# RWKV block: receptances projected last, decays summed on TensorE, preparation folded into the projections

## What is computed

```python
xx = pad(x)[:, :-1] - x                       # the token before, minus this one
xr, xw, xk, xv, xa, xg = [x + xx * mu[i] for i in range(6)]
r, k, v = xr @ w_rkv[0], xk @ w_rkv[1], xv @ w_rkv[2]
w = -softplus(-(w_decay0 + tanh(xw @ w_decay1) @ w_decay2)) - 0.5
a = sigmoid(a0 + (xa @ a1) @ a2)
g = sigmoid(xg @ g1) @ g2
kk = heads(k * k_k);  kk = kk * rsqrt(max(sum(kk * kk), 1e-24))
k = k * (1 + (a - 1) * k_a)
decay = exp(-exp(w))                          # = exp(-c * sigmoid(...)), c = exp(-0.5)
S = S * decay + (S @ -kk) (kk * a)^T + v k^T  # per token and head; y = S @ r
y = groupnorm(y) + sum(r * k * r_k) * v       # the second term is the "bonus"
out = (y * g) @ w_o
```

## Time and profile before

| | |
|---|---|
| median of 3 runs | 2507.64 us |
| profiled execution | 2511.72 us, its span 2509.9 us |
| mean granted TensorE clock | 0.902 |
| PE busy over the span | 2208.5 us, 88% |
| DVE, ACT, POOL busy | 891.5, 981.8, 903.5 us |
| chain that ended last | PE 51%, DVE 8%, ACT 3% |

### The profile page before, as it was taken

One profiled execution on the slowest core, in us unless ns is written; L12 is line 12 of the kernel. 1 busy time (PEld: TensorE's weight loads), 2 busy tenths in 40 slices (PEclk: granted clock), 3 DMA queues, 4 the chain that ended last, 5 costly groups with the idle time before them and its releaser, 6 DMA issues.

```text
span 2509.9 us, 31732 instructions
## 1 busy us (share of the span) xinstructions
PE 2208.5 (88%) x12568; PEld 1736.1 (69%) x12570; DVE 891.5 (36%) x1895; ACT 981.8 (39%) x1833; POOL 903.5 (36%) x582
## 2 busy tenths in 40 slices
PE   5999799999976799963799779999897899999898
PEld 4898666778744567632688467888687657888687
DVE  2100366320076455078243544333104063334301
ACT  3331177442353444332234335344225264434312
POOL 2332066444312233342000343544443393454443
PEclk9988599999997799956589889999999899999999
DMA  4322000133300222201100122333322202333322
GB/s 118 85 63 76 18 27 1 60 78 104 89 18 17 63 63 78 61 1 28 32 26 10 44 84 76 93 93 101 103 98 67 76 2 75 93 93 95 106 91 77
DMA packets 222421, 162.13 MB, mean 65 GB/s; under 512 B 31450, under 2 KB 206114, under 8 KB 222274
## 3 DMA queue, kind: packets, MB, share of 16 engines
q1 hardware_dynamic: 219762, 151.91, 20.6%
q0 software_dynamic: 2512, 8.19, 1.1%
HBM read 154.83 MB, written 5.24 MB: 64 GB/s over the span
## 4 chain that ended last, share of the span: by engine, by line
PE 51%; DVE 8%; ACT 3%; issue 2%; POOL 2%; DMA 1%; POOLq 1%; DVEq 0%; ACTq 0%; SPq 0%; PEld 0%; PEldq 0%
PE ps L358 11%; PE ps L329 8%; PE ps L328 8%; PE ps L332 8%; PE ps L368 5%; PE ps L2594 2%; PE ps L2552 2%; POOL buffer L2070 1%; ACT buffer L2649 1%; POOLq L2910 1%; DVE buffer L2220 1%; PE ps L2617 1%; PE ps L2243 1%; PE ps L2564 1%; POOL weights_lo L270 1%
## 5 line engine op out<-in xcount | busy, mean ns | idle before, releaser
L270 POOL TENSOR_TENSOR weights_lo<-buffer,weights_hi 128x1024 fp32r<-128x1024 f32 (+1 forms) x265 | 656.8, 2481 | 1030.9 <-ACT weights_hi L259 1030.5
L259 ACT ACTIVATE weights_hi<-buffer 128x1024 fp32r<-128x1024 f32 (+1 forms) x265 | 276.0, 1045 | 319.6 <-PE ps L368 310.7
L328 PE MATMUL ps<-u_hi,weights_hi 128*128 128x512 f32 (+1 forms) x752 | 281.5, 378 | 6.4 <-DVE u_lo L644 5.9
L329 PE MATMUL ps<-u_lo,weights_hi 128*128 128x512 f32 (+1 forms) x752 | 285.1, 383 | 0.0
L1801 ACT ACTIVATE buffer<-ps,buffer 128x512 f32<-128x512 f32 x88 | 68.4, 777 | 282.6 <-PE ps L332 282.6
L332 PE MATMUL ps<-u_hi,weights_lo 128*128 128x512 f32 (+1 forms) x752 | 176.7, 378 | 0.0
L1831 DVE SCALAR_TENSOR_TENSOR buffer<-ps,buffer,buffer 128x511 f32<-128x511 f32 x88 | 66.1, 751 | 291.9 <-ACT buffer L1801 291.9
L328 PEld LDWEIGHTS ps<-u_hi,weights_hi 128*128 128x128 f32 x752 | 143.4, 191 | 33.2 <-DVE u_lo L644 6.5
L329 PEld LDWEIGHTS ps<-u_lo,weights_hi 128*128 128x128 f32 x752 | 143.1, 190 | 29.3
L2649 ACT ACTIVATE buffer<-ps 32x128 f32<-32x128 f32 (+4 forms) x240 | 92.5, 392 | 177.4 <-PE ps L2594 60.8
L332 PEld LDWEIGHTS ps<-u_hi,weights_lo 128*128 128x128 f32 x752 | 136.6, 190 | 26.6 <-POOL weights_lo L270 0.3
(11 more groups left out here) (371 smaller groups left out, 4588.7 us busy)
## 6 DMA issues: line engine op xcount, KB each, us to landing
buffer<-in_w_up SPq DMA_DIRECT2D x88, 512.0 KB, 3.8
buffer<-in_w_down SPq DMA_DIRECT2D x44, 512.0 KB, 3.2
buffer<-in_diff_w_in SPq DMA_DIRECT2D x32, 512.0 KB, 4.1
buffer<-in_nsa_w_in SPq DMA_DIRECT2D x28, 512.0 KB, 3.7
buffer<-in_w_rkv SPq DMA_DIRECT2D x24, 512.0 KB, 3.7
buffer<-in_nsa_w_out SPq DMA_DIRECT2D x8, 512.0 KB, 3.5
buffer<-in_diff_w_out SPq DMA_DIRECT2D x8, 512.0 KB, 3.5
buffer<-in_norm_g POOLq DMA_DIRECT2D x8, 512.0 KB, 4.3
```

The source lines that it names most:

```text
L259: self.nc.scalar.activation(self.part_hi[:, part % self.PARTS, 0:n], self.raw[:, ld % self.RAW, 0:n], ACT.Copy).then_inc(self.hi_ready, 1)
L270: self.nc.gpsimd.tensor_tensor(self.part_lo[:, part % self.PARTS, 0:n], self.raw[:, ld % self.RAW, 0:n], self.part_hi[:, part % self.PARTS ...
L328: nc.tensor.matmul(out, hi[:, k, :], rhs[0][:, k, tokens], start=(k == 0), stop=False)
L329: nc.tensor.matmul(out, hi[:, k, :], rhs[1][:, k, tokens], start=False, stop=False)
```

## The change

RwkvPrepare and RwkvDecay are gone; RwkvProject goes straight into RwkvCore.

- The order of projections is now decay, key, a, gate, the two second layers, values, receptances. The mixes have buffers laid out anew, so that the value mix does not share one with the mix before it.
- The decay's second layer is made token-major (65 rows: the bias comes as a row of weights beside a row of ones), so that the prefix sums can be products with a constant triangle matrix less the middle's (`C_SUMS`), made by TensorE straight into PSUM. ScalarE takes both exponents from PSUM into PSUM banks 6 and 7, and the products read them there.
- The values come in two halves of 512 features, 4 loads each. `project_tokens` calls `between` after each load: 32 two-column products give the decay sums at the chunk middles (`mids`), 32 more the squared norms (`squares`).
- The receptance tiles come last. Ahead of each, TensorE makes that tile's decay sums (4 products) and spreads the inverse norms over 64 features each (8 products). VectorE makes all products but kk * a, which stays on GpSimd.
- The bonus sums move into the core: GpSimd makes r * k at its start, TensorE four two-column products at the end of iterations 4 to 11, VectorE copies them out.

```diff
-C_ONES = C_INCL_T + P
+C_SUMS = C_INCL_T + P
...
+    c[:, C_SUMS:C_SUMS + P] = 1.0 * (r[:, None] <= r[None]) - 1.0 * (r[:, None] < P // 2)
...
+        if between:
+            between(index)
...
+        big_hi, s4_lo = env.take_r("mix_w_hi", KD, T, at=env.big_at), env.take_r("mix_w_lo", KD, T, at=slot(4))
+        s2_hi, s3_lo = env.take_r("mix_k_hi", KD, T, at=slot(2)), env.take_r("mix_k_lo", KD, T, at=slot(3))
+        big_lo = env.take_r("mix_v_lo", KD, T, at=env.big_at)
+        self.mixes = [[big_hi, s4_lo], [s2_hi, s3_lo], [big_hi, s4_lo], [s2_hi, s3_lo],
+                      [env.take_r("mix_v_hi", KD, T, at=slot(0)), big_lo],
+                      [env.take_r("mix_r_hi", KD, T, at=env.uT_at), big_lo]]
...
-    MIXES = [1, 2, 4, 0, 5, 3]
+    MIXES = [1, 2, 4, 5, 3, 0]
+    V, R = 4, 5
+    SUMS, SPREAD, SHRINK, GROW = 4, 5, 6, 7
...
+        for rows in (io["decay_rows"], io["a2_2"][0]):
...
+        self.v = [load_tokens(env, w[2], 512 * half, 512) for half in range(2)]
+        self.r = load_features(env, w[0], 0, D)
...
+    def tensor(self, pe):
+        env, nc, m = self.env, self.env.nc, self.m
+        mixed = lambda n: lambda k: pe.wait_ge(self.mix_ready, KD * n + k + 1)
+        for n, lds in enumerate(([self.w1], self.k, [self.a1], self.g1)):
+            for ld, g in lds:
+                project_features(env, pe, ld, m.mixes[n], g, env.loads[ld][2], mixed(n) if ld == lds[0][0] else None)
+        (ld, g), (ld_a, g_a) = self.second
+        pe.wait_ge(env.proj_taken, self.w1[1] + 1)
+        pe.wait_ge(self.row_put, 1)
+        env.wait_whole(pe, ld)
+        for n in range(2 * NT):
+            i, half = n // 2, n % 2
+            env.wait_bank(pe, g + n)
+            nc.tensor.matmul(env.bank(g + n), m.tanh_w[0:65, i * P:(i + 1) * P], env.whole(ld)[0:65, 0, 512 * half:512 * half + 512],
+                             start=True, stop=True).then_inc(env.proj_ready, 1)
+        pe.wait_ge(env.proj_taken, self.a1[1] + 1)
+        env.wait_whole(pe, ld_a)
+        for k in range(KD):
+            env.wait_bank(pe, g_a + k)
+            nc.tensor.matmul(env.bank(g_a + k), env.whole(ld_a)[0:64, 0, k * P:(k + 1) * P], m.hid_a[0:64, :],
+                             start=True, stop=True).then_inc(env.proj_ready, 1)
+        select = env.const[:, C_HEADSEL:C_HEADSEL + 2]
+        def mids():
+            pe.wait_ge(env.proj_taken, g_a + KD)
+            for k in range(KD):
+                for i in range(NT):
+                    at = 2 * (NT * k + i)
+                    mm = nc.tensor.matmul(env.ps[:, 0, at:at + 2], m.decay_rows[:, k, i, :], select, start=True, stop=True)
+            mm.then_inc(self.mids_ready, 1)
+        def squares(k):
+            pe.wait_ge(self.sq_ready, k + 1)
+            for i in range(NT):
+                at = 2 * (NT * k + i)
+                mm = nc.tensor.matmul(env.ps[:, 1, at:at + 2], m.kk_squares[k % 2][:, i * P:(i + 1) * P], select,
+                                      start=True, stop=True)
+            mm.then_inc(self.ss_ready, 1)
+        def beside(half):
+            def between(index):
+                n = NT * half + index
+                if n == 0:
+                    mids()
+                elif n <= NT:
+                    squares(2 * n - 2)
+                    squares(2 * n - 1)
+            return between
+        for half, (lds, gv) in enumerate(self.v):
+            ready = (lambda index: pe.wait_ge(self.mix_ready, KD * self.V + 2 * index + 2)) if half == 0 else None
+            project_tokens(env, pe, lds, m.mixes[self.V], gv, elsewhere=0 if half else 2 * KD, ready=ready,
+                           between=beside(half))
+        pe.wait_ge(env.proj_taken, self.r[0][1])
+        pe.wait_ge(self.norm_ready, 1)
+        pe.wait_ge(self.mids_taken, 1)
+        def decay_sums(k):
+            if k:
+                pe.wait_ge(self.shrink_ready, k)
+                pe.wait_ge(self.grow_ready, k)
+            for i in range(NT):
+                mm = nc.tensor.matmul(env.ps[:, self.SUMS, i * P:(i + 1) * P], m.decay_rows[:, k, i, :],
+                                      env.const[:, C_SUMS:C_SUMS + P], start=True, stop=True)
+            mm.then_inc(self.sums_ready, 1)
+        def spread(k):
+            if k:
+                pe.wait_ge(self.kk_ready, k)
+            for i in range(NT):
+                for st in range(2):
+                    at = 2 * (NT * k + i) + st
+                    mm = nc.tensor.matmul(env.ps[64 * st:64 * st + 64, self.SPREAD, i * P:(i + 1) * P],
+                                          m.inv_norm[:, at:at + 1].to_broadcast([P, DH]), env.ident, start=True, stop=True)
+            mm.then_inc(self.spread, 1)
+        for k, (ld, g) in enumerate(self.r):
+            decay_sums(k)
+            spread(k)
+            project_features(env, pe, ld, m.mixes[self.R], g, ready=mixed(self.R) if k == 0 else None)
 
...
+                if n == self.V and k == 1:
+                    dve.wait_ge(env.proj_ready, self.a1[1] + 1)
...
+        for k in range(KD):
+            mix(self.R, k)
+        step(v.tensor_tensor(m.head_r_k, env.const[:, C_HEADSEL:C_HEADSEL + 2].unsqueeze(1).to_broadcast([P, KD, 2]),
+                             env.vec[:, V_B + 32:V_B + 40].unsqueeze(2).to_broadcast([P, KD, 2]), ALU.mult))
+        dve.wait_ge(self.ss_ready, KD)
+        step(v.tensor_scalar(m.inv_norm, env.ps[:, 1, 0:2 * NT * KD], 1e-24, None, ALU.max))
+        v.reciprocal(m.inv_norm, m.inv_norm).then_inc(self.inv_ready, 1)
+        dve.wait_ge(env.proj_ready, self.r[0][1])
+        for k in range(KD):
+            low(self.R, k)
+        chunks = lambda x: x.rearrange("p (c t) -> p c t", c=NT)
+        grow, shrink = env.ps[:, self.GROW, :], env.ps[:, self.SHRINK, :]
+        for k, (_, g) in enumerate(self.r):
+            kk = m.kk[:, k, :]
+            dve.wait_ge(self.mix_ready, KD * self.R + k + 1)
+            dve.wait_ge(self.spread, k + 1)
+            v.scalar_tensor_tensor(kk, m.k[:, k, :], env.vec[:, V_B + 16 + k:V_B + 17 + k], env.ps[:, self.SPREAD, :],
+                                   ALU.mult, ALU.mult).then_inc(self.kk_ready, 1)
+            dve.wait_ge(self.weight_ready, k + 1)
+            dve.wait_ge(self.kk_ready, k + 1)
+            v.tensor_tensor(m.k[:, k, :], env.pair_tmp[:, k % 2, :], m.k[:, k, :], ALU.mult).then_inc(self.weight_taken, 1)
+            dve.wait_ge(self.grow_ready, k + 1)
+            dve.wait_ge(self.weight_taken, k + 1)
+            v.tensor_tensor(m.k[:, k, :], m.k[:, k, :], grow, ALU.mult)
+            dve.wait_ge(self.turned_b, k + 1)
+            v.tensor_tensor(m.a[:, k, :], m.a[:, k, :], grow, ALU.mult).then_inc(self.grow_taken, 1)
+            dve.wait_ge(self.shrink_ready, k + 1)
+            e, kk = chunks(shrink), chunks(kk)
+            v.scalar_tensor_tensor(kk[:, :, 1:P], kk[:, :, 1:P], -1.0, e[:, :, 0:P - 1], ALU.mult, ALU.mult)
+            v.scalar_tensor_tensor(kk[:, :, 0], kk[:, :, 0], -1.0, m.epos[:, k, :], ALU.mult, ALU.mult)
+            v.tensor_tensor(m.coef[:, k, 1:NT], m.coef[:, k, 1:NT], e[:, 0:NT - 1, P - 1], ALU.mult)
+            dve.wait_ge(env.proj_taken, g + 1)
+            v.tensor_tensor(m.r[:, k, :], m.r[:, k, :], shrink, ALU.mult).then_inc(self.shrink_taken, 1)
 
+        nc.gpsimd.memset(m.tanh_w[64:65], 1.0).then_inc(self.row_put, 1)
+        pool.wait_ge(self.row_put, 1)
+        env.split_lo(pool, self.r[1][0])
+        for k in range(KD):
+            if k + 2 < KD:
+                env.split_lo(pool, self.r[k + 2][0])
+            pool.wait_ge(self.kk_ready, k + 1)
+            pool.wait_ge(self.weight_ready, k + 1)
+            nc.gpsimd.tensor_tensor(m.a[:, k, :], m.a[:, k, :], m.kk[:, k, :], ALU.mult).then_inc(self.turned_b, 1)
...
+        def square(k):
+            if k >= 2:
+                act.wait_ge(self.ss_ready, k - 1)
+            nc.scalar.activation(m.kk_squares[k % 2], m.k[:, k, :], ACT.Square, scale=col(2, k)).then_inc(self.sq_ready, 1)
+        def take_v(half):
+            for i in range(NT):
+                act.wait_ge(env.proj_ready, self.v[half][1] + i + 1)
+                nc.scalar.activation(m.v[:, i, 512 * half:512 * half + 512], env.ps[:, 4 + i, :],
+                                     ACT.Copy).then_inc(env.proj_taken, 1)
...
+        high(self.V, 0)
+        high(self.V, 1)
...
+        (_, g), (_, g_a) = self.second
         for n in range(2 * NT):
+            i, half = n // 2, n % 2
+            if n + 2 < KD:
+                high(self.V, n + 2)
             act.wait_ge(env.proj_ready, g + n + 1)
+            nc.scalar.activation(m.decay_rows[:, 4 * half:4 * half + 4, i, :], env.bank(g + n).rearrange("p (k f) -> p k f", f=P),
+                                 ACT.Sigmoid).then_inc(env.proj_taken, 1)
+        (v0, _), (v1, _) = self.v
+        env.split_hi(act, v0[1])
         for k in range(KD):
+            act.wait_ge(env.proj_ready, g_a + k + 1)
```

(54 more changed lines are left out.)

248 lines of the change are left out of this document (48 added, 200 removed).

## The result

Over 11 runs the changed kernel takes 2489.4 us (2473.2 to 2496.9) against 2509.5 (2504.2 to 2514.7) for the kernel before, 20.1 us faster by the medians; the ratio is 0.9915 with a 95% interval of 0.9902 to 0.9928, which makes 21.3. The forecast was 2479.5, its range 2460 to 2499. So sign and range hold. Some executions run in a slower state whatever the kernel; the ratios leave them out, which concerns two of the last experiment's six alone.

What follows compares the result with a forecast made beforehand. TensorE was taken to bound most of the kernel, except 79.8 us in RwkvPrepare and RwkvDecay. Removing these and a 4.8 us gap, less added terms from +1.9 to +17.7, summed to -28.1: 2479.5 us, range 2460 to 2499.

Steps and rivals of the forecast that it cites:

- Stage up to the core: Projections to core entry: the core's first matmul about 37 us earlier than 1145.4, 28 plus 9 for the bonus.
- the second layers: Decay and a, before the values: +2.5 us on 14.0, from ScalarE's work and a wait for the second value load.
- The value stretch: Value projection with 64 small products added, +15.4 us on TensorE: about 60 us plus the clock's share.
- sums and spread: Decay sums and inverse-norm spreading on TensorE beside the receptances: 2.2 us per tile, +17.7 us in all.
- The entry: Start of the receptance stretch: +3.0 us, 1 for copying the last value banks, 2 for the last mix's low parts.
- the tail: After the last receptance matmul: +1.9 us for a ScalarE copy, a VectorE product, two handoffs and one barrier.
- The handoff rival: Receptance tiles bound by handoffs, 10 us a tile instead of 7.8: +17.6 us, kernel 2497; chance 10%.
- clock holds: Clock stays up through the small products, so the +7 us go: 2472.5, or 2468 with half the bonus hidden; 15%.
- Bonus in the core: Thirty-two two-column products, one group of four at the end of iterations 4 to 11: +9.0 us, 5 if some fall into gaps.
- the last rival: Slower: the bonus keeps core iterations 5 to 11 at half clock, +40 us, kernel 2519; chance 6%.
- the four signs named as right: Receptance tiles 7.8 us apart; value stretch about 60 plus clock share, with dip; second layers 16 to 17; iterations 5-11 at 12.2.
- queue-bound stage: Waits on the in-order ScalarE queue undo the overlap, with a handoff-bound receptance stretch: together 28 us, kernel 2507; chance 6%.

Runs made afterwards that it cites:

- the last experiment: Changed kernel with 32 unused columns put back behind its constants: median 2496.0 us of six (2472.3 to 2520.8), ratio 0.9911 from the four shortest.
- the padded kernel: 32 unused columns behind the constants, added to the changed kernel whose bonus products stand as one group before the first Y: 2470.3 us, ratio 0.9834.
- the early group: Changed kernel with all 32 bonus products as one group ahead of the core's first Y, instead of in iterations 4 to 11: 2450.4 us, ratio 0.9764.

## Why the prediction was right or wrong

**Stage up to the core: right.** Forecast 37 us shorter. From the stage's first matmul to the core's it is 279.1 us before and 235.6 after, 43.5 less, but this mixes in where buffers lie and the course of the clock. Like with like, it is 38.2 less with the old placement (240.9, the padded kernel) and 36.3 to 41.3 less with the short constants' (276.9 in the kernel before with its 96 columns; 235.6 or 240.6 changed). The core's first matmul stands 53.2 us earlier where 37 was forecast, since 9.7 more come from ahead of the stage.

Term by term: the second layers take 16.9 us in the changed kernel, 19.3 in others, for a forecast of 14.0 + 2.5 + 1.5 = 18.0. The value stretch takes 66.1 us; the forecast makes it 46.4 - 1.8 for the cold start + 15.4 + 5.5 = 65.5. The mids took 10.3 (forecast 7.7 + 3.7), a square 0.21 (0.24). The receptance tiles stand 7.59 apart (7.8 forecast), and sums and spread take 2.0 of that (2.2). The entry costs 0.8 us of idle TensorE and 1.2 in the first tile (3.0 forecast), the tail 9.20 - 7.59 = 1.6 (1.9). VectorE is busy for 5.4 us a tile, within the forecast 4.5 to 6.5, although the one full product whose operands both lie in SBUF takes 1.43 us on average and those that read PSUM 0.68 to 0.74. The handoff rival (10 us a tile) is out, and so is "clock holds": clock 0.89 in the value stretch.

**Bonus in the core: the step that failed.** "Seven groups at 0.96 and one at half clock" made +9.0. The own length was right (12.1 against 11.26 us for an iteration at full clock). The reading that the three iterations before the fourth take 16.94 us too is off by 1.0 for iteration 1 (18.0), which changes nothing. The term priced no clock for the iterations around the groups, and that costs some 30 us more: +43.3 in the profiled execution, 38.0 by the groups alone in the kernel before, 39.0 by taking them out of the changed one. This is the last rival, given 6% and a price of +40. The reason against it, "one group of 0.96 in 11.3 us is a small dilution", was wrong. The row in favour, busy for 4.00 of 4.00 us at clock 0.50 two iterations earlier, was the one to weigh: it showed that TensorE can be fully busy in this core and still at half clock, so busy time could not be the reason to expect 11.3 us from iteration 5 on.

**A term that was not there: placement, about -20.** The constants get 32 columns shorter, and the prediction gave that nothing. By the medians it is worth 20.0 us in the padded kernel with the early group and 21.1 in the kernel before. In the profiled executions it shows in two places. The stage begins at 859.0 to 861.5 in the seven other kernels with the short constants and at 864.0 to 866.3 in all those with the constants of before (860.0 in the kernel before with its 96 columns); the changed kernel's 856.6 is ahead of all of them. And from the last Y to the end are 1103.4 to 1107.9 us with the short constants and 1116.4 to 1121.7 with the old ones. Inside the stage it is 2.2 us in the kernel before, and nothing that can be told from the clock in the changed one.

**The sum as the runs have it.** The padded kernel with the early group is the change without its groups in the core and without its placement. Its median lies 42.2 us under that of the kernel before. Placement takes off 20.0 more, and the groups in place add 39.0: -23.2, measured -20.1 (the kernel before itself moves by 3 us from one series of runs to the next). The forecast of -28.1 came near because an omitted gain of 20 stood against an underestimated loss of 30; with these two set right, its own sum gives -18.1. To that extent the hit is luck. By these parts what the change says it does gains about 3 us, since its own two parts, -42 and +39, nearly cancel, and the whole measured gain can be had by 96 unused columns in the kernel before. The direct test does not settle it: the padded changed kernel has its median 14.3 us under the kernel before and two of six executions above it.

**What would have shown it:** of the four signs named as right, three came (tiles, value stretch with its dip, second layers 16.9, though 19.3 in other executions), and of those named as wrong, "core iterations of 17 us go on past the fourth" came as well. The rival of a handoff-bound or queue-bound stage needed no run: the windows show TensorE busy.

## What to carry to other kernels

A group of thin matmuls that is moved into a stretch with TensorE fully busy can have two prices, its length and the clock of everything around it; here they made 39 us, of which the clock had some 30. Look for stretches with TensorE fully busy at clock 0.5 next to stretches of the same work at 1.0, and put thin products where TensorE idles anyway; a few wide products with no use can pay for themselves there. When a diff changes the size of anything that is allocated early, compare one plain matmul's duration far away from the change before crediting the time to the change.

## What the runs showed of the hardware

- Same number of products, about the same length, other columns: four fp32 products of 128x128 by 2 or by 128 columns lengthen an iteration by 0.8 or 0.9 us at full clock (11.3 to 12.1 or 12.2), but the kernel is 26 us faster with 128, and the clock comes up in iteration 6 instead of coming and going.
- Six 128x512 bfloat16 products per iteration, about 1.4 us of added work, take iterations from 17.0 to 12.0 us by raising the clock; 18 of them ahead of the loop bring nothing that can be measured (2453.8 us against 2450.4).
- Of the 128x512 matmuls of the projections some take 0.227 or 0.232 us from start to start by where an operand's buffer lies: 32 columns (128 bytes) of shift, or 96 in the other kernel, move the time by 20.0 and 21.1 us in 2500; the profiled executions show 16.4 and 21.5 us of this kind outside the core. Which distance counts, and why, was not tried.
- Without a filler or groups the clock of the core rises with iteration 5 in most profiled executions, once with iteration 4 and once with 6. Why iterations 1 to 3 stay mostly at half clock stays open; that the second inverse, which ends about there on VectorE, has a part in it was not tested.
